# Two-block transformer step: the opening by feature quarters, with the modulation weights stationary and both token blocks fetched first

## Chip, cores and metric

One core of a Trainium2 chip runs the kernel. The metric is the device time of one execution in microseconds.

## What is computed

Two transformer blocks over 256 tokens of 1024 features follow one another. The change touches only the start of the first one. Its layer begins, for the tokens `x` and for the context `ctx` (256 tokens each), with

```
mod_lat = jnp.split(jax.nn.silu(c) @ w_ada[l] + b_ada[l], 6, axis=-1)
mod_ctx = jnp.split(jax.nn.silu(c_ctx)[None, :] @ w_ada[l] + b_ada[l], 6, axis=-1)
sh1, sc1, gt1, sh2, sc2, gt2 = mod_lat
sh1c, sc1c, gt1c, sh2c, sc2c, gt2c = mod_ctx
pl = project(modulate(rmsnorm(x, g_mix[l]), sh1, sc1), w_in[l], w_dec_up[l], b_dec[l])
pc = project(modulate(rmsnorm(ctx, g_mix[l]), sh1c, sc1c), w_in[l], w_dec_up[l], b_dec[l])
```

where `modulate(h, shift, scale)` is `h * (1 + scale) + shift` by feature, and `project` multiplies by `w_in` (queries, keys, values, gates, a convolution's inputs, and 32 columns `dd` that `w_dec_up` expands into decays). A gated linear attention in both directions over chunks of 64 tokens, a convolution branch and a SwiGLU follow; then the second block with two attentions and two SwiGLUs. All is float32.

## The kernel before

**Products.** A float32 product with weights of `w_in` is made of three: weights and activations are each split into a high part (rounded by ScalarE, `whi`, `A_hi`, `B_hi`) and a remainder (a subtraction on VectorE, `wlo`, `A_lo`, `B_lo`), and high x high, high x low and low x high are summed in PSUM (`three`, L1274). A is the tokens' side, B the context's. A "unit" is 256 columns of a weight matrix, 1 MiB; unit u lives in slot u % 3 of the rings `raw`, `whi`, `wlo`. SP (the queue that issues most transfers) loads it (`load_unit`), ScalarE and VectorE each `split` it, TensorE multiplies. The order of the units is `P1` (L43): dd is unit 0, k0 and k1 are 1 and 2, v0 to v3 are 3 to 6, q0 and q1 are 7 and 8; dd, k and v run for both sides.

**The opening (L1737 to 1771 on TensorE).** Shift and scale of the first norm are 2048 columns of `w_ada`, fetched as eight blocks of 256 columns (`ada0`, 1 MiB each) at the head of SP's queue, with the small vectors behind the second and `ctx` and `x` behind the fourth. For each block TensorE keeps two columns (silu of `c` and `c_ctx`) stationary and streams the block's 256 columns, eight products deep. That gives rows; ScalarE copies them to `arow`, and 16 small transposes (L1756) make columns of them, one for each feature group of 128. VectorE's `columns` adds the biases and the norm's gain. In between run the norms: squares on ScalarE, the root on GpSimd (`norm`, L695), the scaling on VectorE, transposes on TensorE (L1340). Then come shift and scale (`modulate` on ScalarE for ctx, `affine` on VectorE for x), the split into high and low, the dd unit, and k0, whole unit after whole unit.

**Behind it.** `gla(u, half)` (L1469) puts attention steps between the halves of the units: after the first half of k0 and of k1, `decay_products` (L1371) expand dd into decay arguments. ScalarE and VectorE make decays of them (`gla_front`: absolute value, exponential, logarithm, scans), each in program order with the splits of coming units. After the first half of v2 and of v3 TensorE transposes the decayed keys of the context and of the tokens (`turn_keys`, L1387), which ScalarE copies out (`ctx_key_tokens`, `key_tokens`).

**Later modulation.** The other norms' shift and scale are computed by GpSimd and VectorE (`adapt`) from further blocks of `w_ada`, and are brought into columns by `shift_and_scale` (L1357): 16 products with 128 columns stationary and a single column of ones moving.

```
for x in range(2):
    for k in range(KD):
        c = UC * ada_pos(NORM_UNITS[n][x]) + P * k
        ins = mm(bank[b][:, KD * x + k:KD * x + k + 1], acc[:, c:c + P], one, True, True)
```

GpSimd's program starts with the norms' roots, then sets constants, then waits for `as_mm` (the transposed rows) to load its first `w_ada` block, and for `hlo_done` 16 to compute with it.

## Time and profile before

| | us |
|---|---|
| median of 3 runs | 1217.5 (1215.88 to 1219.05) |
| profiled execution | 1218.4 |
| its span | 1216.6 |
| TensorE busy | 1166.5 (96%) |
| VectorE busy | 853.4 (70%) |
| ScalarE busy | 574.0 (47%) |
| GpSimd busy | 325.1 (27%) |

A row of the trace begins with the start in us and the duration, then engine, source line and operation, what it writes and reads, the shapes, and how many instructions it merges; behind it in brackets stands the idle time before it and what ended it. PE is TensorE's products and PEld its weight loads, which overlap; DVE is VectorE, ACT ScalarE, POOL GpSimd. A float32 product shows as two rows ("passes"), a product of split parts as one, a transpose as one. PEclk is the clock granted to TensorE as a share of 2.4 GHz; 0.50 is 1.2 GHz. A row of windows has the stretch and its length, the busy time (and instructions) of PE, PEld, DVE, ACT and POOL, then PEclk, the share of the DMA engines and GB/s. Lines L1272, L838 and L1819 are helpers that record many operations: go by the tiles.

### The profile page before, as it was taken

How to read it: one execution, taken by the hardware profiler on the slowest of the kernel's cores; microseconds unless marked ns; L12 is line 12 of the kernel's file. 1: busy time of each engine (PE TensorE's matmuls, PEld its weight loads, DVE VectorE, ACT ScalarE, POOL GpSimd, SP SyncE). 2: the span in 40 equal slices, each digit the busy share in tenths (PEclk: the TensorE clock that was granted, in tenths of full speed). 3: DMA queues.
4: the chain of work that ended last, by engine and by line, in shares of the span. 5: the costliest groups of instructions: out<-in, count | busy, mean ns of one | idle time of the engine just before them, and what ended most of it. 6: DMA issues, size and time to landing. Idle time of an engine off the chain costs nothing.

```text
span 1216.6 us, 18692 instructions
## 1 busy us (share of the span) xinstructions
PE 1166.5 (96%) x7600; PEld 1040.7 (86%) x7600; DVE 853.4 (70%) x935; ACT 574.0 (47%) x734; POOL 325.1 (27%) x219
## 2 busy tenths in 40 slices
PE   6899999999999899999989999999999989999996
PEld 2599988999999888888878888889998989888885
DVE  0478474489577778877778877788766587755676
ACT  1566434354443364444555444445654625544452
POOL 1376573066565200000020000011156663000000
PEclk9899999999999899999989999999999989999999
DMA  9643645365866648777747777755954655656670
GB/s 310 218 139 105 208 144 168 105 217 186 273 232 218 203 169 275 242 254 257 267 147 255 254 252 246 261 161 190 298 181 149 201 186 179 204 177 201 213 258 35
DMA packets 192354, 250.59 MB, mean 206 GB/s; under 512 B 4763, under 2 KB 171870, under 8 KB 192158
## 3 DMA queue, kind: packets, MB, share of 16 engines
q1 hardware_dynamic: 183838, 217.44, 54.9%
q0 software_dynamic: 8448, 32.18, 7.7%
q8 instruction: 50, 0.82, 0.3%
q14 instruction: 18, 0.15, 0.0%
HBM read 248.56 MB, written 1.05 MB: 205 GB/s over the span
## 4 chain that ended last, share of the span: by engine, by line
PE 77%; DVE 13%; ACT 4%; issue 3%; SPq 2%; DMA 1%; POOL 0%; POOLq 0%; DVEq 0%; ACTq 0%
PE twin L1272 74%; DVE arena L1819 4%; DVE wlo L1819 3%; ACT arena L838 2%; DVE arena L1827 2%; SPq L564 1%; DMA raw<-in_w_in 1%; ACT whi L838 1%; PE twin L1340 1%; DVE X L1819 1%; DVE A_both L1819 1%; PE twin L1607 0%; DVE B_lo L1819 0%; DVE X L1827 0%; ACT L838 0%
## 5 line engine op out<-in xcount | busy, mean ns | idle before, releaser
L1272 PE MATMUL twin<-A_both,whi 128*128 128x256 f32 (+1 forms) x2224 | 584.7, 340 | 2.5 <-DVE arena L1819 1.1
L1819 DVE TENSOR_TENSOR wlo<-raw,whi 128x2048 fp32r<-128x2048 f32 x170 | 422.0, 2484 | 158.9 <-ACT whi L838 158.8
L1272 PE MATMUL twin<-A_both,wlo 128*128 128x256 f32 x1640 | 440.1, 281 | 0.0
L838 ACT ACTIVATE whi<-raw 128x2048 fp32r<-128x2048 f32 x170 | 325.1, 1912 | 217.9 <-PE twin L1272 212.1
L1272 PEld LDWEIGHTS twin<-A_both,whi 128*128 128x128 f32 x2224 | 375.1, 191 | 45.9 <-issue 6.7
L1272 PEld LDWEIGHTS twin<-A_both,wlo 128*128 128x128 f32 x1640 | 312.3, 190 | 11.3 <-DVE A_both L1819 0.4
L838 ACT ACTIVATE arena<-twin 128x512 f32<-128x512 f32 (+6 forms) x168 | 88.8, 554 | 125.5 <-PE twin L1272 84.8
L838 ACT ACTIVATE arena<-arena 128x512 f32<-128x512 f32 (+7 forms) x132 | 70.0, 559 | 164.3 <-DVE arena L1819 128.6
L756 POOL TENSOR_TENSOR ada_raw<-ada_raw,arena 128x2048 f32<-128x2048 f32 x24 | 104.7, 4361 | 145.9 <-DMA ada_raw<-in_w_ada 135.0
L1272 PE MATMUL twin<-whi,A_both 128*128 128x256 f32 x640 | 123.9, 295 | 15.4 <-DVE A_both L1819 10.3
L1272 PE MATMUL twin<-whi,B_hi 128*128 128x512 f32 (+2 forms) x340 | 126.8, 373 | 0.2 <-DVE B_lo L1819 0.2
L1272 PE MATMUL twin<-arena 128*2 128x256 f32 (+11 forms) x752 | 115.8, 318 | 11.3 <-DMA arena<-in_w_ada 11.1
L1272 PE MATMUL twin<-wlo,B_hi 128*128 128x512 f32 (+2 forms) x340 | 125.2, 368 | 0.0
L1272 PE MATMUL twin<-whi,B_lo 128*128 128x512 f32 (+2 forms) x340 | 125.2, 368 | 0.0
L1272 PEld LDWEIGHTS twin<-whi,A_both 128*128 128x128 f32 x640 | 105.2, 202 | 17.2 <-DVE A_both L1819 10.7
L1272 PEld LDWEIGHTS twin<-arena 128*128 128x128 f32 (+6 forms) x752 | 79.6, 155 | 39.4 <-issue 15.6
L1819 DVE TENSOR_TENSOR arena<-arena,twin 128x512 f32<-128x512 f32 x92 | 62.3, 684 | 62.4 <-ACT arena L838 49.3
L720 POOL TENSOR_SCALAR arena<-arena 128x1 f32<-128x1 f32 x4 | 1.6, 393 | 375.4 <-ACT arena L838 375.3
L1827 DVE SCALAR_TENSOR_TENSOR arena<-ada_raw,arena 128x256 f32 (+1 forms) x196 | 95.1, 485 | 7.0
L1272 PE MATMUL twin<-wlo,A_both 128*128 128x256 f32 x320 | 93.4, 292 | 0.0
L1272 PEld LDWEIGHTS twin<-whi,B_lo 128*128 128x128 f32 x340 | 64.2, 189 | 11.3 <-issue 0.7
L1272 PEld LDWEIGHTS twin<-wlo,B_hi 128*128 128x128 f32 x340 | 64.2, 189 | 10.7
(128 smaller groups left out, 1203.7 us busy)
## 6 DMA issues: line engine op xcount, KB each, us to landing
raw<-in_w_in SPq DMA_DIRECT2D x49, 1024.0 KB, 5.8
raw<-in_ffn_w_in SPq DMA_DIRECT2D x44, 1024.0 KB, 5.1
ada_raw<-in_w_ada POOLq DMA_DIRECT2D x28, 1024.0 KB, 6.2
ada_raw<-in_w_ada SPq DMA_DIRECT2D x24, 1024.0 KB, 5.4
raw<-in_w_ffn_in SPq DMA_DIRECT2D x22, 1024.0 KB, 5.1
raw<-in_ffn_w_out SPq DMA_DIRECT2D x22, 1024.0 KB, 5.0
raw<-in_w_ffn_out SPq DMA_DIRECT2D x11, 1024.0 KB, 5.1
arena<-in_w_ada SPq DMA_DIRECT2D x8, 1024.0 KB, 11.9
```

Source lines behind the costliest of these rows:

```text
L564: sp.dma_start(ada0[j], a["w_ada"][0].rearrange("(p k) n -> p k n", k=KD)[:, :, UC * j:UC * j + UC])\
L720: link(nc.gpsimd.tensor_scalar(p[0], p[0], EPS, None, ALU.add))
L756: link(nc.gpsimd.tensor_tensor(v[:], v[:], c3[:, :, s:s + 1].to_broadcast([P, KD, UC]), ALU.mult))
L838: return nc.scalar.activation(o, i, f, **kw)
L1272: return nc.tensor.matmul(o, l, r, start=start, stop=stop, **kw)
L1340: ins = nc.tensor.transpose(bank[norm_bank(n, b)][:, c:c + P], src[:, t, P * k:P * k + P], ident)
L1819: return nc.vector.tensor_tensor(o, x, y, op)
L1827: return nc.vector.scalar_tensor_tensor(out=o, in0=x, scalar=sc, in1=y, op0=op0, op1=op1)
```

## The change

- SP's order is `ctx`, the small vectors, `x`, then `w_ada` blocks 0, 4, 1, the dd unit, k0, and blocks 5, 2, 6, 3, 7. The dd unit is fetched 128 columns wide instead of 256, and only its 32 used columns are split.
- The work goes by four quarters of the features (two groups of 128). Block q holds the shift and block q + 4 the scale of quarter q. `start_columns` on TensorE makes columns directly: the block's 128 columns of weights are stationary, and the two columns of `c3` move; 16 products for a block. Rows, `arow` and its transposes are gone.
- For each quarter VectorE makes shift and scale, ScalarE (ctx) and VectorE (x) apply them, and split. TensorE adds that quarter's part of the dd product (`decay_part`, 12 products) and of all of k0 (`key_part`, 24 products).
- ScalarE and VectorE split k1 (`split(2)`) ahead of the fourth quarter.
- `decay_products` for the first two groups come after all of k0 instead of after its first half. The key transposes and their copies come one unit later (context) and half a unit to a unit later (tokens).
- GpSimd sets its constants ahead of the two norms, and its first `w_ada` load waits for the last columns.

```diff
         if n == 0:
-            b = [0, 7] if kind == "dd" else [0]
+            b = [0]
...
+                width = P if kind == "dd" else UC
+                return cview(w, c0 + UC * n, width), KD, width
...
-            for j in range(8):
-                if j == 2:
-
...
+            def load_start(j):
                 sp.dma_start(ada0[j], a["w_ada"][0].rearrange("(p k) n -> p k n", k=KD)[:, :, UC * j:UC * j + UC])\
                     .then_inc(start_ada[j], 16)
-                if j == 3:
-                    sp.dma_start(ctxX, a["ctx"].rearrange(tok, p=P)).then_inc(x_in[0], 16)
-                    sp.dma_start(X[:], a["x"].rearrange(tok, p=P)).then_inc(x_in[1], 16)
+
+            sp.dma_start(ctxX, a["ctx"].rearrange(tok, p=P)).then_inc(x_in[0], 16)
+            for name, r0 in VEC.items():
+                v = a[name]
+                n = math.prod(v.shape) // P
+                src = bass.AP(tensor=v.tensor, offset=0, ap=[[P, n], [1, P]])
+                sp.dma_start(vrows[r0:r0 + n, :], src).then_inc(vec_in, 16)
+            for name, r0, n in (("b_ada", 0, 48), ("b_ada_2", 48, 72)):
+                src = bass.AP(tensor=a[name].tensor, offset=0, ap=[[P, n], [1, P]])
+                sp.dma_start(brows[r0:r0 + n, :], src).then_inc(vec_in, 16)
+            sp.dma_start(X[:], a["x"].rearrange(tok, p=P)).then_inc(x_in[1], 16)
+            load_start(0)
+            load_start(4)
+            load_start(1)
+            load_unit(0, *P1[0])
+            load_unit(1, *P1[1])
+            for j in (5, 2, 6, 3, 7):
+                load_start(j)
 
             for u, (kind, n) in enumerate(P1):
-                load_unit(u, kind, n)
+                if u >= 2:
+                    load_unit(u, kind, n)
...
+        def dd_part(v):
+            return v[:, 0:KD * P].rearrange("p (k w) -> p k w", k=KD)[:, :, 0:2 * RANK]
+
...
+        def start_turned(n, q):
+
+            return 2 * n + q + 1 if q < 2 else 2 * q + n + 1
+
         def norm_bank(n, b):
 
-            return {0: (4, 5, 6, 0), 1: (1, 2, 3, 4), 2: (5, 6, 7, 2), 5: (4, 6, 7, 2)}.get(n, (4, 5, 6, 2))[b]
+            return {0: (1, 2, 1, 2), 1: (4, 7, 4, 7), 2: (5, 6, 7, 2), 5: (4, 6, 7, 2)}.get(n, (4, 5, 6, 2))[b]
 
...
-                    pool.wait_ge(as_mm, 1)
+                    pool.wait_ge(start_cols, 4)
...
+            def start_quarter(q):
+
+                h, ks = start_h[1][q], slice(2 * q, 2 * q + 2)
+                act.wait_ge(start_mod, q + 1)
+                act.wait_ge(tr_done, start_turned(0, q))
+                for m in range(2):
+                    k = 2 * q + m
+                    ins = run(h[:, m, :], bank[norm_bank(0, q)][:, T * m:T * m + T], ACT.Identity,
+                              bias=shift[:, 1, k:k + 1], scale=scale[:, 1, k:k + 1])
+                ins.then_inc(h_done, 1)
+                act.wait_ge(h_done, q + 1)
+                run(B_hi[:, ks, :], h).then_inc(hhi_done, 1)
+                act.wait_ge(h_dve, q + 1)
+                run(A_hi[:, ks, :], start_h[0][q]).then_inc(hhi_done, 1)
+
...
-                if u == U_V + 2:
+                if u == U_V + 3:
                     for g in range(4):
                         ctx_key_tokens(g)
-                if u == U_V + 3:
+                if u == U_Q:
                     for g in range(4):
                         key_tokens(g)
 
...
-            act.wait_ge(ada0_mm, 1)
-            run(arow[:, 0:512], bank[0][0:2, :]).then_inc(ada0_row, 1)
             squares(1)
-            for b in range(1, 4):
-                if b == 3:
-                    split(0)
-                    split(1)
-                act.wait_ge(ada0_mm, b + 1)
-                run(arow[:, 512 * b:512 * b + 512], bank[b][0:2, :]).then_inc(ada0_row, 1)
-            modulate(0)
-            modulate(1)
+            act.wait_ge(landed[0], 16)
+            run(dd_part(whi[0]), dd_part(raw[0])).then_inc(hi_ready, 1)
+            start_quarter(0)
+            split(1)
+            start_quarter(1)
+            start_quarter(2)
+            split(2)
+            start_quarter(3)
 
             for u in range(N1):
                 if u:
                     evac1(u - 1)
-                split(u + 2)
+                    split(u + 2)
...
-                if (u, half) == (U_V + 2, 0):
+                if (u, half) == (U_V + 3, 0):
                     pe.wait_ge(ek_done, 4)
                     for g in range(4):
                         turn_keys(g, Eb[g], ktc_tr)
-                if (u, half) == (U_V + 3, 0):
+                if (u, half) == (U_V + 3, 1):
                     for g in range(4):
                         pe.wait_ge(ktc_sb, g + 1)
                         turn_keys(g, Lb[g], kt_tr)
...
+            def start_columns(j):
+
+                x, q = divmod(j, 4)
+                if q and x == 0:
+                    pe.wait_ge(start_mod, q)
+                pe.wait_ge(start_ada[j], 16)
+                for m in range(2):
+                    c = 2 * (KD * x + 2 * q + m)
+                    for k in range(KD):
+                        ins = mm(bank[3][:, c:c + 2], ada0[j][:, k, P * m:P * m + P], c3[:, k, 0:2],
+                                 k == 0, k == KD - 1)
+                if x:
+                    ins.then_inc(start_cols, 1)
+
+            def start_turn(n, *quarters):
+
+                src = norm_source(n)
+                for t in range(TT):
+                    pe.wait_ge(xn_done, 2 * n + t + 1)
+                    for q in quarters:
+                        if q >= 2:
+                            pe.wait_ge((h_done, h_dve)[n], q - 1)
+                        for m in range(2):
+                            k = 2 * q + m
+                            c = T * m + P * t
+                            ins = nc.tensor.transpose(bank[norm_bank(n, q)][:, c:c + P], src[:, t, P * k:P * k + P],
+                                                      ident)
+                        if t == TT - 1:
+                            ins.then_inc(tr_done, 1)
+
+            def decay_part(q):
+
+                wh, wl = dd_part(whi[0]), dd_part(wlo[0])
+                if q == 0:
+                    pe.wait_ge(lo_ready, 1)
+                    pe.wait_ge(vec_done, 1)
+                for s, x in ((1, B), (0, A)):
+                    pe.wait_ge(hlo_done, 4 * q + (2 if s else 4))
+                    for k in (2 * q, 2 * q + 1):
+                        ins = three(bank[0][0:2 * RANK, T * s:T * s + T], (wh[:, k, :], wl[:, k, :]),
+                                    (x[0][:, k, :], x[1][:, k, :]), True, k == 0 and s == 1, k == KD - 1,
+                                    skip_group_check=True)
+                if q == 3:
+                    ins.then_inc(unit_used, 1)
+
+            def key_part(q):
+
...
+                b = BANKS1[1]
+                for x, o in ((B, bank[b[1]]), (A, bank[b[0]])):
+                    for half in range(2):
+                        for k in (2 * q, 2 * q + 1):
+                            ins = step_product(1, o[:, T * half:T * half + T], x, half, False, k,
+                                               k == 0 and half == 0, None, False)
+                if q == 3:
+                    ins.then_inc(unit_used, 1)
+
             pe.wait_ge(c_silu, 1)
-            for j in range(8):
-                if j == 4:
...
-                if j == 6:
-                    norm(0)
-                pe.wait_ge(start_ada[j], 16)
-                for k in range(KD):
-                    ins = mm(bank[j // 2][0:2, UC * (j % 2):UC * (j % 2) + UC], c3[:, k, 0:2], ada0[j][:, k, :],
-                             k == 0, k == KD - 1)
...
-            norm(1)
+            pe.wait_ge(ident_done, 1)
+            pe.wait_ge(vec_in, 16 * (len(VEC) + 2))
+            nc.tensor.transpose(bank[6][:, 0:NVEC], vrows[0:NVEC, :], ident[0:NVEC, 0:NVEC])
+            nc.tensor.transpose(bank[6][:, P:P + BROWS], brows[0:BROWS, :], ident[0:BROWS, 0:BROWS])\
+                .then_inc(vec_tr, 1)
+            start_turn(0, 0, 1)
+            start_columns(0)
+            start_turn(1, 0, 1)
+            start_columns(4)
+            start_columns(1)
+            decay_part(0)
+            start_columns(5)
+            key_part(0)
+            start_columns(2)
+            start_turn(0, 2)
+            start_turn(1, 2)
+            decay_part(1)
+            start_columns(6)
+            key_part(1)
+            start_columns(3)
+            start_turn(0, 3)
+            start_turn(1, 3)
+            start_columns(7)
+            decay_part(2)
+            key_part(2)
+            decay_part(3)
+            key_part(3)
+            gla(U_K, 0)
 
...
+            def start_columns(q):
+
+                k = slice(2 * q, 2 * q + 2)
+                v = bank[3][:, 0:32].rearrange("p (x k s) -> p x s k", x=2, s=2)
+                both = [P, 2, 2]
+                dve.wait_ge(start_cols, q + 1)
+                if q == 0:
+                    dve.wait_ge(vec_done, 1)
+                tt(shift[:, :, k], v[:, 0, :, k], bcol[:, 2 * q:2 * q + 2].unsqueeze(1).to_broadcast(both), ALU.add)
+                c = KD + 2 * q
+                link(tt(scale[:, :, k], v[:, 1, :, k], bcol[:, c:c + 2].unsqueeze(1).to_broadcast(both), ALU.add))
+                g = VEC["g_mix"] + 2 * q
+                stt(scale[:, :, k], scale[:, :, k], 1.0, vec[:, g:g + 2].unsqueeze(1).to_broadcast(both),
+                    ALU.add, ALU.mult).then_inc(start_mod, 1)
+
+            def start_quarter(q):
+
+                ks = slice(2 * q, 2 * q + 2)
+                start_columns(q)
+                dve.wait_ge(start_mod, q + 1)
+                dve.wait_ge(tr_done, start_turned(1, q))
+                for m in range(2):
+                    k = 2 * q + m
+                    ins = ts(start_h[0][q][:, m, :], bank[norm_bank(1, q)][:, T * m:T * m + T],
+                             scale[:, 0, k:k + 1], shift[:, 0, k:k + 1], ALU.mult, ALU.add)
+                ins.then_inc(h_dve, 1)
+                for s, (hi, lo) in ((1, (B_hi, B_lo)), (0, (A_hi, A_lo))):
+                    dve.wait_ge(hhi_done, 2 * q + (1 if s else 2))
+                    rest(lo[:, ks, :], start_h[s][q], hi[:, ks, :]).then_inc(hlo_done, 2)
+
...
-            split(0)
-            dve.wait_ge(vec_done, 1)
-            columns(0, 7, VEC["g_mix"], 0, (0, 1))
-            for b in range(4):
-                low(0, b)
-                dve.wait_ge(tr_done, 4 + b + 1)
-                for k in (2 * b, 2 * b + 1):
-                    ins = affine(1, k)
-                ins.then_inc(h_dve, 1)
-            for b in range(4):
-                low(1, b)
+            dve.wait_ge(hi_ready, 1)
+            rest(dd_part(wlo[0]), dd_part(raw[0]), dd_part(whi[0])).then_inc(lo_ready, 1)
+            start_quarter(0)
             split(1)
+            start_quarter(1)
+            start_quarter(2)
+            split(2)
+            start_quarter(3)
 
             for u in range(N1):
                 if u:
                     evac1(u - 1)
 
                 gla_step(2 * (u - 1 - U_Q) + 1)
-                split(u + 2)
+                if u:
+                    split(u + 2)
```

## Rows read from the trace of the kernel before

**Rows 1.** The page: span, engines' busy times, TensorE's clock in 40 slices.

```profile
span 1216.6 us, 18692 instructions
...
PE 1166.5 (96%) x7600; PEld 1040.7 (86%) x7600; DVE 853.4 (70%) x935; ACT 574.0 (47%) x734; POOL 325.1 (27%) x219
...
PEclk9899999999999899999989999999999989999999
```

**Rows 2.** Timeline of TensorE in the opening: start us, duration us, instruction, count.

```profile
9.12 16.45 PE L1272 MATMUL twin<-arena 128*2 128x256 f32 x64 [9.12 <-DMA arena<-in_w_ada]
...
14.19 10.88 PEld L1272 LDWEIGHTS twin<-arena 128*2 128x2 f32 x51 [0.29 <-issue]
...
45.40 0.90 PE L1756 MATMUL twin<-arena,ada_raw 2*128 2x2 f32 x12
...
51.68 0.56 PE L1272 MATMUL twin<-B_hi,whi 128*128 128x256 f32 x1
...
67.90 3.72 PE L1272 MATMUL twin<-arena 32*128 32x256 f32 x16
```

**Rows 3.** Timeline of three engines behind the opening, and one row of windows.

```profile
69.07 3.43 ACT L838 ACTIVATE arena<-twin,arena 128x256 f32<-128x256 f32 x8 [5.50 <-PE twin L1272]
...
119.56 2.28 DVE L1819 TENSOR_TENSOR wlo<-raw,whi 128x2048 fp32r<-128x2048 f32 x1
...
122.03 0.47 PE L1272 MATMUL twin<-whi,A_both 128*128 128x256 f32 x2 [3.10 <-ACT arena L838]
...
120.00:125.00 5.00, 2.97 (x19) 3.00 (x20) 5.00 (x5) 5.00 (x8) 4.63 (x3) 0.84 0.35 104
```

**Rows 4.** Timeline of SP, ScalarE and VectorE in the opening.

```profile
3.57 1.15 SPq L560 DMA_DIRECT2D arena<-in_g_mix  x1
...
8.16 1.25 SPq L564 DMA_DIRECT2D arena<-in_w_ada  x2
...
41.40 1.91 ACT L838 ACTIVATE whi<-raw 128x2048 fp32r<-128x2048 f32 x1 [4.20 <-DMA raw<-in_w_in]
...
44.78 1.91 ACT L838 ACTIVATE whi<-raw 128x2048 fp32r<-128x2048 f32 x1 [1.47 <-DMA raw<-in_w_in]
...
47.73 0.24 DVE L1819 TENSOR_TENSOR arena<-twin,arena 128x8 f32<-128x8 f32 x2 [2.10 <-PE twin L1756]
...
50.34 0.69 DVE L1819 TENSOR_TENSOR B_lo<-arena,B_hi 128x512 fp32r<-128x512 f32 x1 [1.82 <-ACT B_hi L838]
...
50.95 0.99 DVE L1824 TENSOR_SCALAR arena<-twin,arena 128x256 f32<-128x256 f32 x2
```

**Rows 5.** Timeline of TensorE: three places with the passes of `shift_and_scale`.

```profile
420.29 3.65 PE L1272 MATMUL twin<-arena 128*128 128x1 f32 x32
...
811.01 3.63 PE L1272 MATMUL twin<-arena 128*128 128x1 f32 x32
...
1014.09 3.63 PE L1272 MATMUL twin<-arena 128*128 128x1 f32 x32
```

**Rows 6.** Windows around these places and in the opening, and transposes behind one.

```profile
55.00:56.00 1.00, 0.99 (x7) 0.79 (x6) 1.00 (x3) 0.75 (x3) 0.00 (x0) 0.94 0.00 0
...
424.00:426.00 2.00, 2.00 (x11) 2.00 (x11) 0.38 (x4) 0.00 (x0) 0.18 (x1) 0.50 1.09 371
...
811.00:813.00 2.00, 2.00 (x20) 1.99 (x18) 1.93 (x4) 1.14 (x4) 0.68 (x2) 1.00 0.90 356
...
1017.60:1019.00 1.40, 1.40 (x9) 1.40 (x9) 1.07 (x4) 0.00 (x0) 0.87 (x1) 0.53 1.00 381
...
423.80 3.58 PE L1340 MATMUL twin<-arena 128*128 128x128 f32 x16
```

**Rows 7.** Timeline of TensorE's weight loads in the opening, two single loads.

```profile
52.05 0.33 PEld L1272 LDWEIGHTS twin<-B_hi,wlo 128*128 128x128 f32 x1
...
55.24 0.19 PEld L1272 LDWEIGHTS twin<-B_hi,wlo 128*128 128x128 f32 x1
```

**Rows 8.** Timeline of GpSimd: the head norm of the attention.

```profile
244.10 0.30 POOL L683 TENSOR_SCALAR arena<-arena 128x4 f32<-128x4 f32 x1 [45.74 <-ACT arena L838]
```

110 lines of the change are left out of this document (23 added, 87 removed).

## Prediction

> **What bounds the kernel now.** Of the page I read first the shares and the slices [rows 1]: TensorE is busy for 96% of 1216.6 us, and only the first two of 40 slices fall short (6 and 8 tenths, clock 9 and 8 tenths). So the rest is TensorE's own time, and an opening that is N us shorter or longer moves everything behind it by N, unless a wait further on takes it up. The timeline of the opening shows what it is made of [rows 2]: TensorE starts at 9.12 when the first block of w_ada lands, and is in w_ada passes, transposes and waits until 51.68, when the decay product starts. At 67.90 come the first `decay_products` (16 passes over 32 rows).
>
> That 67.90 is my **reference point**, because a serial chain starts there: ScalarE's Abs, Exp and Ln from 69.07, VectorE's scans, up to the low half of unit 5's weights at 119.56; TensorE resumes at 122.03 after 3.10 us idle [rows 3]. From 67.90 to 122.03 are 54.1 us, in which TensorE has 51.0 us of work. Before the change the second half of k0 lies in it (48 products, 5.8 us at 0.12, more at the low clock); after it all of k0 lies ahead of the reference point. The chain does not get shorter by that: the idle time at unit 5 grows from 3.1 to some 9 or 10 us, and unit 5 starts 54.1 us behind the reference point in both kernels. Hence: **change of the time = shift of the first `decay_products`**.
>
> **When the weights come.** The first block of w_ada (1 MiB) is used at 9.12; the dd unit, the eleventh MiB, at 41.40, the k0 unit at 44.78, both by a ScalarE that had waited for them [rows 2, 4]. That is (41.40 - 9.12)/10 = 3.23 us for each MiB. The two token blocks now come first, so the first w_ada block lands third: 9.12 + 2 x 3.23 = 15.6. SP issues eleven small transfers between ctx and x, which took 4.6 us of it (3.57 to 8.16) [rows 4]; one MiB covers only 3.2 of these, and I put the first w_ada block at 16.6 (15.6 to 17.6). The last block is at 11.5 MiB: 43.9 to 46. Transfers of MiB 3 to 12 arrive every 3.2 us.
>
> **TensorE's part, step by step.** The eight w_ada blocks cost 128 passes of 0.213 us before (51 in 10.88, at full clock), 27 us [rows 2]. Now each block is 16 products with 128 columns of weights stationary and two columns moving. The nearest row is `shift_and_scale`, the same with one moving column: 16 products stand as 32 passes and take 3.63 to 3.65 us, 0.114 each, at full clock [rows 5]. Eight blocks: 8 x 3.65 = 29.2 us. So at full clock the column products win nothing over the row products, but drop the transposes of `arow` and the last copy between them (45.40 to VectorE's first use at 47.73, 2.3 us) [rows 2, 4].
>
> But the clock does not stay full. Behind the stretches at 420.29 and 1014.09 the granted clock halves: 0.50 in 424 to 426, 0.53 in 1017.6 to 1019 [rows 5, 6]. TensorE was issuing passes without a gap, and it halved all the same. In the opening it also begins at the low level: the first 13 of 64 passes take 16.45 - 10.88 = 5.6 us, 0.43 each, twice the later 0.213 [rows 2]. In the new order there are column stretches from the first block on, with few dense products between them, so I take the opening to be at the low level (1.2 GHz) except behind dense pieces.
>
> What does a column pass cost there? No row shows one. From below it is 0.114 (if the load does not slow down), 3.65 a block; from above double, 7.3. The nearest rows are single loads of 128 columns: 0.33 us at the low level (52.05), 0.19 at the full one (55.24) [rows 7]. The load is longer by 0.14, more than a whole pass of 0.114, so I take it to double. I take 0.216, just under the double: 6.9 a block.
>
> The Trainium skill, page "TensorE: Matmul & The Clock Gate", section "LDWEIGHTS (loading the stationary operand)", states that a load takes its columns over 1.2 GHz, with no mention of the clock level. By that (an estimate) the low level would leave the block at 3.65, and the sum below would give 74 to 77 rather than 91. The load's 0.33 against 0.19 speaks against it [rows 7]. It is the second rival.
>
> The sum at the low level, from 16.6: columns 8 x 6.9 = 55.3; 24 transposes at 0.224 (16 took 3.58) = 5.4 [rows 6]; decay product 4 x 12 and k0 4 x 24, 144 products of 256 columns, which stream for 0.213 as above, with their step 0.215 = 31.0; TensorE waits twice about 0.8 us, once for the first quarter's shift and scale (VectorE's operations from 47.73 on [rows 4]), once for the dd evacuation ahead of `decay_products` = 1.6. End 109.9. The eight transposes of ctx fall into the wait for the first block. At full clock, everything but the columns halved: 16.6 + 29.2 + 24 x 0.112 + 144 x 0.12 + 1.6 = 67.4.
>
> Dense pieces bring the clock back: in the decay product it rose at about 55.1 (0.94 over 55 to 56) [rows 6]. Once full, it stays so through most of a stretch of columns of 3.65 us (420.29 to 423.94) [rows 5], and each us at full clock does the work of two. Four dense pieces lie between the blocks (12 products, 24, 12, 24): I count 3.4 us for each, 13.6. The last piece is 72 products without a block between: 4.5 us at the low level (21 products), then 51 x 0.12 = 6.1 instead of 11.0, 4.9 saved (0.12 is the 0.215 at twice the clock, and a little). 109.9 - 13.6 - 4.9 = **91.4**.
>
> **The other parts.** *VectorE and ScalarE* need, for a quarter, the shift and scale (about 0.6), two affines 0.99, and a hi and two los on 512 columns, 0.7 each: 3.7 us [rows 4], under TensorE's next blocks; only the last one could show, and 36 products (7.7 us) stand before its first use. *ScalarE's `split(2)`* waits ahead of the fourth quarter for the k1 weights, 12.5 MiB, at about 48; TensorE reaches the seventh column block after 75, so nothing waits for that. Without this cover it would cost, see the fifth rival. *The narrower dd unit* saves half a MiB and most of one split (2.3 us VectorE, 1.9 ScalarE): hidden. *GpSimd*: constants ahead of the norms, a few us, in its idle time before the norms. Its first ada load waits for the last columns rather than `as_mm`, so it slides with TensorE by about as much; its slack is 45.7 us idle before the head norm at 244.10 [rows 8]. *The key transposes* go one unit later (32 of them, the same work). The second set is now copied by ScalarE in q0, behind v3's evacuation and one split (1.91 [rows 4]), and its first user comes in q1, 5.8 us of products later. Cost nothing; if that cover were gone, 1 to 2 us. In the idle time at unit 5 the clock falls, but it did so before (0.84 in 120 to 125) [rows 3].
>
> **Result.** Shift 91.4 - 67.9 = +23.5. The profiled execution was 1218.4 with a span of 1216.6, and becomes 1241.9; the median of the runs shown is 0.9 lower: **1241**.
>
> **The rivals.** (1) The forecast: low clock, loads doubled. If two more or two fewer pieces lift the clock, 1234 to 1248; with the start at 15.6 or 17.6, one more either way: 1233 to 1250. Chance 0.57. (2) Low clock, but loads keep their time: a block costs 3.65, the sum at the low level is 16.6 + 29.2 + 5.4 + 31.0 + 1.6 = 84, less four pieces of dense work only (about 1 us each) and 4.9: 74 to 77, +6 to +9, 1223 to 1227. For it: no row shows a column pass at the low level; against: the load's duration. 0.20. (3) The clock stays full, since dense products lie among the columns: dense products end at 811.01, and it stood at 1.00 over 811 to 813, all columns [rows 5, 6]. Reference point 67.4: 1217, no change. Against: the start has no dense work for some 15 us. 0.08. (4) The clock never comes back before the last piece: 109.9 - 4.9 = 105, 1255. 0.06. (5) **Faster**: the transfers, not TensorE, set the end. Last weights at 45 to 48, `split(2)` 1.9 + 2.3 [rows 3, 4], the quarter 3.7, the last 36 products 4.3, the dd evacuation 0.8: 59 to 61, shift -7 at 61, 1210.5. It decides if TensorE's own sum comes to less than 61, that is if a column pass is under 0.09 us and the clock is full; for it, loads that overlap; against, all three rows of 0.114 [rows 5]. 0.09.
>
> **How the numbers follow.** The likeliest is (1), 1241. A range of 1221 to 1251 holds (1) and (2), 0.77, and a little of the cases beside them; I take 1221 to 1252. A measurement of this kernel tells 0.3% (3.7 us) from no change: within it lies (3) and an edge of (2), 0.10; faster is (5), 0.09; slower is the rest, 0.81.
>
> **What the profile after would show.** Column groups (128 x 2 moving) of 32 passes, 6.9 us where the clock reads 0.50, 3.65 where it reads 1.00: this tells (1) from (2). TensorE hardly idle between 17 and 90. First 32-row passes at 91, unit 5's start 54 behind them, with near 10 us idle. The last w_ada block landed 30 us before its use. The prediction is wrong if the clock reads 1.00 over 25 to 70, or if TensorE there waits for w_ada.

## The result and the profile after

The change makes the kernel slower: median 1243.85 us (4 runs, 1241.95 to 1247.81) against 1218.28 (4 runs, 1215.88 to 1220.97) beside it on the same chip, a ratio of 1.0197 (95% interval 1.0164 to 1.0230). The forecast was 1241 in a range of 1221 to 1252. The profiled execution took 1244.9 with a span of 1243.2, 26.6 us above [rows 1].

Lines of the page after (shares, tenths of TensorE's busy time and of its clock in 40 slices):

```profile
PE 1184.7 (95%) x7712; PEld 1078.4 (87%) x7712; DVE 854.8 (69%) x941; ACT 570.8 (46%) x729; POOL 319.9 (26%) x219
...
PE   5998799999999799999989999999999989999997
...
PEclk9979899999999899999989999998999989999999
```

TensorE is again busy 95% of the time; of the 26.6 us, 18.2 are more busy time of its own (1184.7 against 1166.5), although the number of passes is nearly the same. The timeline of TensorE in the opening tells why; its columns are those of [rows 2]:

```profile
15.02 1.11 PE L1754 MATMUL twin<-arena 128*128 128x128 f32 x4 [0.36 <-DVE arena L1877]
15.93 6.82 PE L1272 MATMUL twin<-arena 128*128 128x2 f32 x32
22.61 1.95 PE L1754 MATMUL twin<-arena,X 128*128 128x128 f32 x8
24.35 6.83 PE L1272 MATMUL twin<-arena 128*128 128x2 f32 x32
31.70 6.98 PE L1272 MATMUL twin<-arena 128*128 128x2 f32 x32 [0.52 <-DVE arena L1881]
...
41.09 6.82 PE L1272 MATMUL twin<-arena 128*128 128x2 f32 x32
...
53.03 3.97 PE L1272 MATMUL twin<-arena 128*128 128x2 f32 x32
...
60.77 3.91 PE L1272 MATMUL twin<-arena 128*128 128x2 f32 x32
68.75 3.63 PE L1272 MATMUL twin<-arena 128*128 128x2 f32 x32
...
73.15 5.86 PE L1272 MATMUL twin<-arena 128*128 128x2 f32 x32
...
90.00 3.72 PE L1272 MATMUL twin<-arena 32*128 32x256 f32 x16
```

These are the last transposes of ctx, the eight column blocks with the transposes of x behind the first, and, last, the first `decay_products`. The first four blocks take 6.8 to 7.0 us each, the next three 3.6 to 4.0, the last 5.9: 44.8 us together. The same 32 passes take 0.213 us each in one group and 0.114 in another. Two rows of windows (stretch, busy of PE, PEld, DVE, ACT, POOL, then PEclk, DMA share, GB/s) show the two levels of the granted clock, one between two of the faster blocks, one inside the second of them:

```profile
58.00:60.00 2.00, 2.00 (x11) 1.67 (x10) 0.00 (x0) 0.00 (x0) 0.00 (x0) 0.50 0.00 0
...
62.00:64.00 2.00, 2.00 (x20) 2.00 (x19) 0.00 (x0) 0.00 (x0) 0.00 (x0) 0.99 0.00 0
```

The reference point has moved from 67.90 to 90.00, by 22.1 us, and nothing behind it takes that up. Unit 4 and unit 5 start like this, against the one wait of 3.10 in [rows 3]:

```profile
127.66 0.77 PE L1272 MATMUL twin<-whi,A_both 128*128 128x256 f32 x2 [6.89 <-ACT arena L849]
...
144.80 0.48 PE L1272 MATMUL twin<-whi,A_both 128*128 128x256 f32 x2 [3.38 <-ACT arena L849]
```

Unit 5 is 22.8 us later than before (122.03). From there to 868.12 (845.55 before) the distance stays between 22.5 and 22.8. The other 4 us of the 26.6 arise in the second block's attention and the stage behind it, where the change touches nothing; the experiments come to them.

### The profile page after: what moved, and what is told of

Its sections match the earlier page's. It is cut to its first block, busy times and chain, and to the rows that moved or that the text cites. A ratio compares the mean times of both kernels' runs of the same rounds, so it can differ in the third digit from the quotient of the medians.

```text
span 1243.2 us, 18933 instructions
## 1 busy us (share of the span) xinstructions
PE 1184.7 (95%) x7712; PEld 1078.4 (87%) x7712; DVE 854.8 (69%) x941; ACT 570.8 (46%) x729; POOL 319.9 (26%) x219
## 4 chain that ended last, share of the span: by engine, by line
PE 80%; DVE 13%; ACT 4%; issue 3%; SPq 0%; POOL 0%; DMA 0%; POOLq 0%; DVEq 0%; ACTq 0%
PE twin L1272 77%; DVE arena L1873 4%; DVE wlo L1873 4%; ACT arena L849 2%; DVE arena L1881 2%; ACT whi L849 1%; PE twin L1333 1%; DVE X L1873 1%; DVE arena L2129 0%; DVE arena L2131 0%; PE twin L1754 0%; PE twin L1599 0%; DVE X L1881 0%; DVE A_both L1873 0%; ACT L849 0%
## 5 line engine op out<-in xcount | busy, mean ns | idle before, releaser
L1272 PE MATMUL twin<-A_both,whi 128*128 128x256 f32 (+2 forms) x2224 | 584.5, 340 | 1.2 <-DVE arena L1873 1.1
L1873 DVE TENSOR_TENSOR wlo<-raw,whi 128x2048 fp32r<-128x2048 f32 (+1 forms) x170 | 424.5, 2498 | 165.7 <-ACT whi L849 165.6
L1272 PE MATMUL twin<-A_both,wlo 128*128 128x256 f32 (+1 forms) x1640 | 440.0, 281 | 0.0
L849 ACT ACTIVATE whi<-raw 128x2048 fp32r<-128x2048 f32 (+1 forms) x170 | 323.6, 1904 | 221.5 <-PE twin L1272 212.8
L1272 PEld LDWEIGHTS twin<-A_both,whi 128*128 128x128 f32 (+1 forms) x2224 | 374.0, 190 | 44.8 <-issue 6.8
L1272 PEld LDWEIGHTS twin<-A_both,wlo 128*128 128x128 f32 (+1 forms) x1640 | 311.1, 190 | 11.7 <-DVE A_both L1873 0.6
L1272 PE MATMUL twin<-whi,A_both 128*128 128x256 f32 x640 | 125.6, 298 | 23.2 <-DVE A_both L1873 10.7
L849 ACT ACTIVATE arena<-twin 128x512 f32<-128x512 f32 (+5 forms) x167 | 88.8, 557 | 113.7 <-PE twin L1272 92.2
L1272 PE MATMUL twin<-arena 128*128 128x2 f32 (+9 forms) x880 | 128.6, 302 | 0.5 <-DVE arena L1881 0.5
L1272 PEld LDWEIGHTS twin<-arena 128*128 128x128 f32 (+5 forms) x880 | 113.7, 200 | 9.0 <-DVE arena L1881 0.6
L768 POOL TENSOR_TENSOR ada_raw<-ada_raw 128x1024 f32<-128x1024 f32 x24 | 79.4, 3306 | 1.9
```

The lines of the kernel that those rows point to most:

```text
L768: link(nc.gpsimd.tensor_tensor(v[:, 0:4, :], v[:, 0:4, :], v[:, 4:8, :], ALU.add))
L849: return nc.scalar.activation(o, i, f, **kw)
L1272: return nc.tensor.matmul(o, l, r, start=start, stop=stop, **kw)
L1873: return nc.vector.tensor_tensor(o, x, y, op)
```

## The experiments

My theory: the opening is TensorE's own time, and what makes it long is the low clock, which doubles a column pass (I take its length to be that of its weight load). Rivals: the transfers' new order, the cutting into quarters with its waits, or the chain behind the opening. "Before" beside the runs was 1219.4, 1225.3, 1218.5 and 1223.8 us (medians of 13 runs in each of four sets); single executions of it lie between 1215.7 and 1227.6, and the shortest has a mean granted clock of 0.980, the longest of 0.974. Where only a single time is given, I go by landmarks of the trace rather than by the time.

**Half of the column work.** Each column product is summed over four of its eight feature groups only, so the modulation is left half computed.

```
-                    for k in range(KD):
+                    for k in range(KD // 2):
```

> The changed kernel with the second half of each column product left out (features 4 to 7 of each partition's eight are not summed into shift and scale). Theory (TensorE sets the opening's end, and a column pass costs its weight load): the eight blocks took 44.8 us in the changed kernel, so the first decay_products moves from 90.0 to 65 to 69, and the time falls by 21 to 25 us, to about 1220. Rival (the opening is set by the chain of quarters, or by transfers and the split of k1 ahead of the fourth quarter, not by the columns): the first decay_products stays at 88 to 90, time within 2 us of the changed kernel.

Measured 1212.99 us (about 1220 expected), first decay products at 63.14, 2 us earlier than the theory's range. The blocks, now of 16 passes, on TensorE's timeline:

```profile
15.93 3.41 PE L1272 MATMUL twin<-arena 128*128 128x2 f32 x16
...
38.39 1.84 PE L1272 MATMUL twin<-arena 128*128 128x2 f32 x16
42.41 1.84 PE L1272 MATMUL twin<-arena 128*128 128x2 f32 x16
47.07 1.84 PE L1272 MATMUL twin<-arena 128*128 128x2 f32 x16
49.69 2.46 PE L1272 MATMUL twin<-arena 128*128 128x2 f32 x16
```

Half of the passes is 22.4 us of 44.8, yet the reference point came 26.9 us earlier than in the changed kernel (90.00). The remaining 4.5 us I put down to the clock: from the block at 38.39 on, the third quarter's, it falls back once (the last block takes 2.46 instead of 1.84), where the changed kernel fell back three times (0.50 over 57.2 to 60.5, 64.1 to 67.3 and 74.3 to 84.3 us). The column work carries the loss; with transfers, quarters and waits unchanged, those rivals fall as the main cause.

**Key products behind the decays.** `key_part(0)` to `key_part(3)` leave the quarters and follow in one piece after the first `decay_products`.

```
-            key_part(0)
...
-            key_part(3)
             gla(U_K, 0)
+            for q in range(4):
+                key_part(q)
```

> The changed kernel with all four parts of k0 behind the first decay_products. Theory: 17.5 us of dense products leave the path ahead of the first decay_products, but the clock now has only the short decay parts to come back by, so columns that took 3.6 to 4.0 us take near 6.8 again and give back some 9 us: first decay_products at 80 to 86, time 1232 to 1238. Rival (clock and dense pieces have nothing to do with each other, columns keep their times of 3.6 to 4.0 from the fifth block on): first decay_products at 72 to 74, time about 1224.

Measured 1236.75. TensorE has 96 products less ahead of the reference point, 11.5 us at full clock, and gains 2.4: it comes at 87.55, a little later than the 80 to 86 that I had written, but far from the rival's 72 to 74. The sixth, seventh and eighth block now read

```profile
59.40 6.82 PE L1272 MATMUL twin<-arena 128*128 128x2 f32 x32
66.74 6.99 PE L1272 MATMUL twin<-arena 128*128 128x2 f32 x32 [0.52 <-DVE arena L1879]
...
75.32 6.83 PE L1272 MATMUL twin<-arena 128*128 128x2 f32 x32
```

All eight are at the low level. So it is the pieces of 24 key products that bring the clock back in the changed kernel; the pieces of 12 decay products alone don't here. Dense work among the columns has a price below its own length.

**Rows instead of columns, all else as in the change.** The same quarters, transfers and order; each block is again two silu columns stationary and 256 columns of weights moving, with a copy and four small transposes for each quarter.

```
-                        ins = mm(bank[3][:, c:c + 2], ada0[j][:, k, P * m:P * m + P], c3[:, k, 0:2], ...
+                    ins = mm(bank[0][2 * RANK:2 * RANK + 2, UC * x:UC * x + UC], c3[:, k, 0:2],
+                             ada0[j][:, k, :], k == 0, k == KD - 1, skip_group_check=True)
```

> The changed kernel with the same order of transfers, quarters and units, but each w_ada block again multiplied as rows (two columns stationary, 256 moving), copied by ScalarE for each quarter and turned by four small transposes. Theory (the stationary weights are what costs, since their passes do not hold the clock and are paced by loads): row passes stream and bring the full clock, 3.4 us a block; first decay_products at 69 to 73, time 1219 to 1223. Rival (the tokens ahead of w_ada and the work by quarters cost the 22 us): first decay_products at 85 to 90, time 1238 to 1243.

Measured 1221.86 (1218.44 to 1222.79), ratio 1.0007 (0.9987 to 1.0027): no change against the kernel before. First decay products at 68.39.

```profile
15.94 4.44 PE L1284 MATMUL twin<-arena 128*2 128x256 f32 x16
20.31 1.09 PE L1778 MATMUL twin<-arena,X 128*128 128x128 f32 x8
21.33 3.62 PE L1284 MATMUL twin<-arena 128*2 128x256 f32 x16
...
126.33 0.77 PE L1284 MATMUL twin<-whi,A_both 128*128 128x256 f32 x2 [7.13 <-ACT arena L852]
```

A block is 16 passes here and takes 3.62, and the clock is up within the first (4.44). This is the cleanest split of the change at the reference point: quarters, tokens first and the key products ahead cost 0.5 us; swapping the operands costs the other 21.6. At full clock both forms take the same 3.6 us. What differs is the clock they run at. Further on the split shifts: unit 5 starts at 126.33 behind a wait of 7.13 for ScalarE, 4.3 us later than in the kernel before and 18.5 earlier than in the changed one, so in these three executions some 4 us belong to the new order and the quarters from there on. The spans (1220.6 against 1216.6 and 1243.2) say the same; over all runs the interval leaves room for 3 us at most.

**Filler.** Behind each half block, four products of a matrix of ones with 256 columns of w_ada, into an unused part of the bank (and one wait for the ones at the start).

```
+                    for _ in range(4):
+                        ins = mm(bank[3][:, 128:384], ones[:], ada0[j][:, 0, :], True, True)
```

> The changed kernel with four products of 256 moving columns added behind each of the 16 half blocks of columns: only work added (27 us at the full clock), whose results nobody reads. Theory (the clock falls because column passes stream next to nothing): with streaming among them the clock comes up with the first blocks, every column half block takes 1.8 us (3.6 for a block), and the added work is nearly paid by it: first decay_products at 93 to 99, time 1246 to 1252. Rival (the column passes are slow for another reason than the clock): they stay at 3.4 us a half block wherever they were, first decay_products at 115 or later, time above 1265.

Measured 1250.66, first decay products at 97.92: as expected.

```profile
15.91 3.41 PE L1272 MATMUL twin<-arena 128*128 128x2 f32 x16
19.18 3.76 PE L1272 MATMUL twin<-arena,ones 128*128 128x256 f32 x8
22.74 1.97 PE L1272 MATMUL twin<-arena 128*128 128x2 f32 x16
24.57 1.97 PE L1272 MATMUL twin<-arena,ones 128*128 128x256 f32 x8
```

After the first filler every column pass of the opening is at 0.115 to 0.13: the 16 half blocks take 31.4 us instead of 44.8 (3.41 + 1.97 + 2.08 + 13 x 1.84). The clock fell back once (0.50 over 36.7 to 40), and there it met a filler. The fillers themselves are 35 us, so the exchange doesn't pay, but it turns the clock with the column products, their loads and the transfers unchanged: the low level is the cause of the doubled pass.

**The kernel before with tokens first.** `ctx` and `x` go ahead of the eight w_ada blocks.

```
+            sp.dma_start(ctxX, a["ctx"].rearrange(tok, p=P)).then_inc(x_in[0], 16)
+            sp.dma_start(X[:], a["x"].rearrange(tok, p=P)).then_inc(x_in[1], 16)
             for j in range(8):
```

> The kernel before with only the order of transfers changed: both token blocks ahead of all w_ada blocks. Theory (the order costs by itself only the later start of the row passes, and part of that falls into waits that TensorE had anyway): TensorE's first row pass at 15 to 17 instead of 9.1, first decay_products at 70 to 73 instead of 67.9, time 1221 to 1225. Rival (the order costs the whole 6.5 us, as no wait takes it up): 74.4, time 1226. Second rival (hidden): 68, time as before.

Measured 1223.84 (single). First decay products at 66.48, 1.4 us earlier than before, not 2 to 5 later: TensorE starts at 12.94 instead of 9.12, but from there on waits for no block. The order of the transfers costs nothing in the opening. The span of this execution (1222.0) is 5.4 us longer all the same, though well within what single executions of the kernel before take. About half of it arises at a wait further on (2.80 at 173.19, for two VectorE operations that took 6.88 beside a GpSimd multiplication of 4.66), and the other 3 us right behind that wait, where the granted clock is 0.50 over 174 to 180 against 1.00 at the same work before. The wait belongs to the theory on GpSimd below.

**Columns with w_ada first.** Blocks 0 and 4 are fetched and multiplied ahead of the tokens and the small transposes.

```
+            load_start(0)
+            load_start(4)
             for name, r0 in VEC.items():
...
             pe.wait_ge(c_silu, 1)
+            start_columns(0)
+            start_columns(4)
```

> The changed kernel with w_ada blocks 0 and 4 ahead of the token blocks in SP's queue and on TensorE; all else as changed. Theory: TensorE starts its columns at 9 instead of 15.9 and works without a wait from there, so the first decay_products moves from 90.0 to 83 to 85, time 1236 to 1240. Rival (a later wait, for the small vectors, the tokens' norms or the fifth transfer, takes the gain): 88 to 90, time as changed.

Measured 1238.81; first decay products at 92.71, 8 us later than my theory and 2.7 later than in the changed kernel.

```profile
8.94 13.78 PE L1272 MATMUL twin<-arena 128*128 128x2 f32 x64 [8.94 <-DMA arena<-in_w_ada]
22.58 0.37 PE L1793 MATMUL twin<-arena 75*128 75x75 f32 x1
...
26.40 1.12 PE L1754 MATMUL twin<-arena 128*128 128x128 f32 x4 [3.25 <-DVE arena L1877]
...
31.73 6.83 PE L1272 MATMUL twin<-arena 128*128 128x2 f32 x32
```

TensorE begins 7 us sooner, but the norms need the transposed vectors of 22.58, which now stand behind 13.8 us of columns. TensorE waits for what follows from them (3.25 us ahead of the transposes of ctx, here and in the changed kernel), and the third block starts at 31.73, against 31.70 in the changed kernel. The rival (a later wait takes the gain) was right; the 2.7 us more come behind 31.73 from the same work, at a lower clock (the last block takes 6.82 instead of 5.86).

**Rows, w_ada first, keys last.** Row products, feature quarters, keys behind the decays, and the splits of units 1 and 2 behind the quarters. Against the row variant above:

```
             pe.wait_ge(c_silu, 1)
+            start_rows(0)
+            start_rows(4)
             pe.wait_ge(ident_done, 1)
...
             gla(U_K, 0)
+            for q in range(4):
+                key_part(q)
```

> A version built on what was found: row passes (as before), w_ada blocks 0 and 4 first, work by quarters (as changed), all of k0 behind the first decay_products, splits of k0 and k1 behind the last quarter, k0's weights last among these transfers, split of v0 behind the logarithms. Theory (the chain from the first decay_products sets unit 5's start, so everything not needed for it leaves its path): first decay_products at 50 to 54, unit 5 at 104 to 111 (54 to 57 later; TensorE has as much work in between), time 1202 to 1210. Rival (moving k0 behind it only makes TensorE the bound of that stretch, and the gain is given back): first decay_products at 50 to 54 but unit 5 at 116 or later, time 1212 or more.

Measured 1217.53 (1214.73 to 1221.59), ratio 0.9950 (0.9925 to 0.9975). First decay products at 65.38 instead of the 50 to 54 that I wrote. The cause is that of the run before: rows 0 and 4 end at 18.3, then the norms are waited for, and the third block starts at 28.49. The time is the rival's (1212 or more): at the `shift_and_scale` passes of 420.29 in the kernel before, this one stands at 422.57.

**Rows, tokens first, keys last.** The same in the change's order of transfers and work.

```
             start_turn(0, 0, 1)
+            start_rows(0)
             start_turn(1, 0, 1)
+            start_rows(4)
...
+            for q in range(4):
+                key_part(q)
```

> Row products, feature quarters, transfers and order of work as in the changed kernel (tokens first), all key products behind the first decay products, the splits of units 1 and 2 behind the quarters. My theory, that TensorE's own work sets the first decay products: 68.39 of the row variant with keys between, less 96 key products at 0.12, 11.5, so 56 to 60; then the chain behind it of 54 to 58 us gives a shift of -8 to -11 and 1208 to 1213. The rival, that something else is then last (the chain of ScalarE and VectorE with its splits, as where the row variant had its chain at 57.9 instead of 54.1): first decay products at 56 to 60 as well, but the time at 1214 to 1219.

Measured 1217.00 (1213.65 to 1219.81), ratio 0.9974 (0.9950 to 0.9997). First decay products at 62.80, not 56 to 60, behind two waits for the last quarter:

```profile
50.43 3.62 PE L1287 MATMUL twin<-arena 128*2 128x256 f32 x16
...
58.91 0.30 PE L1287 MATMUL twin<-B_hi,whi 128*32 128x256 f32 x1 [3.03 <-DVE B_lo L1902]
...
62.80 7.16 PE L1287 MATMUL twin<-arena 32*128 32x256 f32 x16 [2.19 <-ACT arena L852]
```

Without the key products, ScalarE's and VectorE's work for the last quarter is uncovered: 5.2 us of waits, and the clock falls in them (the decay products take 7.16 instead of 3.72). In the prediction the last quarter was hidden by 36 products in front of its first use; here that cover is gone, and the price is seen. The time is the rival's.

**The kernel before, opening lengthened.** The last block's row product is made seven times over.

```
+                for _ in range(7 if j == 7 else 1):
                     for k in range(KD):
```

> The kernel before, its last w_ada block's row product made seven times over: 6 x 16 = 96 passes more, 0.213 us each at full clock, 20.4 us, all ahead of the last copy of the rows. My theory, that an opening longer by N makes the whole longer by N and nothing more: first decay products at 88.3, unit 5 at 142.4, time 1238 to 1240 (+20 to +22). The rival, that a late opening costs something further on by itself (the changed kernel's span grew by 26.6 where its opening grew by 22.1): +24 or more, 1242 or above. The other rival, slack behind the opening that takes some of it up: under 1236.

Measured 1239.58 (1234.88 to 1243.43), ratio 1.0161 (1.0104 to 1.0218); the profiled execution 1236.1. First decay products at 85.06, 17.2 us later. That is less than the 20.4 us added, since up to the last pair of blocks this execution was already 2.5 us ahead. All later landmarks:

```profile
138.72 0.47 PE L1272 MATMUL twin<-whi,A_both 128*128 128x256 f32 x2 [2.57 <-ACT arena L838]
...
862.93 0.41 PE L1272 MATMUL twin<-whi,B_hi 128*128 128x384 f32 x1 [0.17 <-DVE B_lo L1820]
...
1008.86 0.79 PE L1272 MATMUL twin<-whi,A_both 128*128 128x256 f32 x2 [4.08 <-DVE A_both L1820]
```

Unit 5 is 16.7 later, 862.93 is 17.4 later, 1008.86 (991.23 before) 17.6, the span 17.5. So in this execution a longer opening passes through one to one, and being late costs nothing by itself. The 4 us more of the changed kernel are something else. The four times fall into two pairs, 1234.9 and 1236.1, 1243.1 and 1243.4; of the upper pair there is no trace. The rival's 1242 or above is what two of the four show, so it is excluded for the traced execution only.

**GpSimd's multiplication in four pieces.** Where they arise, the changed kernel has this on VectorE and GpSimd:

```profile
935.88 5.63 DVE L1873 TENSOR_TENSOR wlo<-raw,whi 128x2048 fp32r<-128x2048 f32 x1
...
935.76 3.61 POOL L767 TENSOR_TENSOR ada_raw<-ada_raw,arena 128x2048 f32<-128x2048 f32 x1 [5.53 <-DMA ada_raw<-in_w_ada]
939.44 4.32 POOL L768 TENSOR_TENSOR ada_raw<-ada_raw 128x1024 f32<-128x1024 f32 x1
...
945.98 0.63 PE L1599 MATMUL twin<-arena 128*128 128x128 f32 x4 [2.14 <-ACT arena L849]
...
989.12 5.68 DVE L1873 TENSOR_TENSOR wlo<-raw,whi 128x2048 fp32r<-128x2048 f32 x1 [0.67 <-ACT whi L849]
...
995.55 0.35 PE L1272 MATMUL twin<-B_hi,whi 128*128 128x256 f32 x1 [1.87 <-DVE B_lo L1873]
```

The split takes 2.28 alone. Begun 0.12 us behind GpSimd's multiplication, it took 5.63: until 939.37, where that ended, and then its own 2.28 (3.49 + 2.28 = 5.77, nearly what was measured). GpSimd's next operation, 2.38 alone, took 4.32 and ended 2.25 behind VectorE's. They don't share a rate; each waits for the other's instruction to end. ScalarE's softmax and TensorE wait behind it. The Trainium skill, page "SBUF — State Buffer", section "Who interferes with whom", states this: an operation of VectorE with two SBUF inputs contends with one of GpSimd that reads SBUF, and the ports that the two engines share are an exclusive lock. The trace agrees (5.63 against 2.28). In the kernel before, the same split came at 913.30, ahead of GpSimd's at 914.83, and took 2.28.

This is not all of the 4 us. The changed kernel is 22.6 us behind at 868.12 and 24.8 at 945.98, of which 0.9 is given back by 967. The same meeting comes again at 989.12 (5.68; the split before took 2.29 at 965.17, begun ahead of GpSimd's), and TensorE's wait at 995.55 is 0.8 longer than its counterpart. Behind this wait the clock falls, and it did not before:

```profile
995.70:999.10 3.40, 3.40 (x18) 3.40 (x19) 3.40 (x4) 0.47 (x1) 3.32 (x2) 0.52 0.90 306
```

The same work in the kernel before, 970.80 to 975.00, has a granted clock of 1.00. That is the last 1.8 us. So about half of the 4 us is the clock; that the longer wait let it fall is likely, but not shown. The edit makes the waits shorter:

```
-                link(nc.gpsimd.tensor_tensor(v[:], v[:], c3[:, :, s:s + 1].to_broadcast([P, KD, UC]), ALU.mult))
+                for k in range(0, KD, 2):
+                    link(nc.gpsimd.tensor_tensor(v[:, k:k + 2, :], v[:, k:k + 2, :], c3[:, k:k + 2, s:s + 1]...
```

> The changed kernel, GpSimd's multiplication of 128x2048 in adapt made in four pieces of 128x512. In the second block's attention VectorE's split of 2.28 us took 5.63 at 935.88, begun 0.12 us behind GpSimd's multiplication of 3.61. Theory, that VectorE waits for the end of a GpSimd instruction that is under way: with pieces of about 1 us no split is above some 4 us, TensorE's wait there of 2.14 us falls to 1.3 or less, and the time to 1240 to 1243. The rival, that the two engines only share a rate over their common time: splits of 5 us and more stay, and the time is 1243 to 1246.

Measured 1240.32 (1239.35 to 1241.37), ratio 1.0163 (1.0118 to 1.0207), 3.5 us below the median of the changed kernel. TensorE's timeline:

```profile
415.14 0.50 PE L1274 MATMUL twin<-whi,A_both 128*128 128x256 f32 x2 [0.57 <-DVE A_both L1875]
...
956.23 0.63 PE L1601 MATMUL twin<-arena 128*128 128x128 f32 x4 [0.86 <-ACT arena L851]
...
1030.83 6.99 PE L1274 MATMUL twin<-arena 128*128 128x1 f32 x32 [9.02 <-POOL arena L772]
```

The wait in the attention is 0.86 instead of 2.14, no split there is above 3.1 us, and at 415.14 a wait of 6.31 (at 422.77 in the changed kernel) has shrunk to 0.57. The kernel gains 8 to 9 us on the changed one up to 844 us, and in the second block's attention and the stage behind it, where the changed kernel lost its 4, it gains on: at 1003.77 it is 18.2 ahead. Then it loses most of this: at 1030.83 TensorE waits 9.02 us for GpSimd's last block, and the passes behind that wait run at the low level (6.99 instead of 3.6). Four pieces take GpSimd 4.4 us where nothing meets them and mostly 6.3, at most 8.8, where VectorE works beside it, instead of 3.6 for the one. The span is 5.6 us shorter than the changed kernel's (1237.6). This opening, the same instructions as the change, also ended 3.0 us later (93.00): its last column block stayed at 6.83 us where the other had 5.86. So much can the clock differ for the same code in the opening.

**Pieces in the first transformer block only**, on the kernel before and on the rows with tokens first.

```
+                w = 2 if n < NADA1 else KD
+                for k in range(0, KD, w):
```

> The kernel before, GpSimd's multiplication of 128x2048 in four pieces of 128x512 for the 16 blocks of w_ada of the first transformer block only. In the changed kernel with pieces everywhere the last product stage of the first block began at 415.14 instead of 422.77, 7.6 us earlier (TensorE's wait for VectorE's A_both 0.57 instead of 6.9), and lost it again at 1030.83, where GpSimd was 9 us late. Theory, that VectorE's waits behind long GpSimd instructions cost TensorE that time in any version: start of the same stage at 393 to 395 instead of 400.06, time 1209 to 1213. The rival, that the gain was a matter of how the engines happened to stand to each other in that one kernel: less than 3 us, 1215.5 or above.

(The 6.9 in that text is 6.31, as above.) Measured 1215.70 (1213.63 to 1218.73), ratio 0.9949 (0.9926 to 0.9972). The stage begins at 397.93, not at 393 to 395. The wait there is 1.54 instead of 6.18, but a new one of 4.65 for VectorE came at 131.73. 2.1 us of the 7.6 are left at that stage: closer to the rival. Behind the shorter wait the clock stays up (1.00 over 397 to 403 us, 0.50 in the kernel before), so that the next `shift_and_scale` passes come 3.6 us earlier (416.74 against 420.29).

> The row variant with tokens first and the key products behind the decays (1217.0, its stage at 398.39), with the same four pieces in the first block. Theory: the two gains add up, 1.5 us from the opening and 5 to 8 from the pieces, the stage at 391 to 393, time 1208 to 1212. The rival, that the pieces' gain depends on how the engines happen to stand: 1215 or above.

Measured 1208.73 (1207.60 to 1214.95), ratio 0.9897 (0.9845 to 0.9949): faster than both kernels, the whole interval below 1. The stage begins at 389.34 after 0.44 us of waiting, 10.7 us earlier than in the kernel before. Against the same kernel without pieces that is 9.1 us (398.39), where the pieces gave the kernel before 2.1. What they bring depends on how the two engines stand to each other; that they bring something held in all three kernels, though by 0.3 to 0.8%, with the runs in part taken in different sets.

## Why the prediction was right, point by point

- **Start of the columns.** 16.6 forecast, 15.93 measured, but not by the way of the forecast, the landing of the first w_ada block. TensorE goes from the transposes of ctx at 15.02, which had waited for VectorE (0.36), into the columns without a wait. So the agreement says little about the sum of the transfers. TensorE waits nowhere for w_ada, and the last block stands ready well before 73.15, since the DMA share is down to 0.03 over 50 to 52 us. As expected; the fifth rival (faster, transfers set the end) would have needed the columns in 0.09 us a pass.
- **A column pass at the low level.** The step between two rows, load kept or doubled: 6.9 a block taken, 6.82 measured, 0.213 a pass against 0.114. The load of [rows 7], longer by 0.14 at the low level, was the right row to go by, and the second rival falls. That the pass is as long as its load is argued, not shown: one and two moving columns take the same 0.114. The rule of the Trainium skill, page "TensorE: Matmul & The Clock Gate", section "LDWEIGHTS (loading the stationary operand)", names columns over 1.2 GHz for a load and no clock level; for a pass that doubles with the level the trace doesn't agree, and the measurement decides. The filler run shows it with nothing else changed: 3.41 for 16 passes at the low level, 1.84 to 1.97 at the full one.
- **How often the clock comes back.** Four pieces at 3.4 us, 13.6 off 55.3, were forecast, so 41.7 for the eight blocks; measured 44.8. The sum is near, the count was not: the first piece (12 products) brought nothing, the three blocks behind the second to fourth piece gained 2.9 to 3.3 each, and the last gained 1.0. In the keys-last run the first two pieces of 12 lifted nothing; here the third piece, also 12, did, begun 1 us behind a stretch at the full level. I had counted all four alike.
- **Last piece.** 72 products in 10.6 and a wait of 0.8 forecast; from 79.01 to 90.00 are 11.0. The step of a product of split parts at the low level is 0.213, near the 0.215 taken; the row pass that the prediction likened it to has that length at the full level.
- **Reference point.** 91.4 forecast, 90.00 measured: +23.5 against +22.1. That it is so near is in part luck: the column blocks took 3 us more than forecast, while start, waits, transposes and products together took 4.5 less.
- **The chain behind it.** 54.1 us forecast to unit 5, measured 54.8; idle time 9 to 10 forecast at unit 5, measured 10.3, but 6.9 of it at unit 4, which waits for ScalarE's copy of k1. The chain was right, its place in part: the row variant had 57.9 there, so 54 is not a constant of the chain.
- **Costed at nothing.** Key transposes, GpSimd's later start, the narrower dd, `split(2)`: between unit 5 and 845.55 the shift stays within 0.3 us, so they cost nothing that shows. But the row variant is 4.3 us behind the kernel before at unit 5 and waits there for ScalarE; the order of ScalarE's work is not free once the opening is short.
- **What was missed.** The sum ends 3.0 us short of the profiled execution (1241.9 against 1244.9), or 2.9 of the median. The opening was 1.4 shorter than forecast, the chain 0.7 longer; the missing term is the 4 us between 868.12 and the end, where VectorE's two-input operations and GpSimd's meet differently and the clock falls once more. "Shift of the time = shift of the first decay products" holds where only the opening is lengthened (17.2 to 17.5). Elsewhere the spans depart from it by up to 7 us: tokens first moved the reference point by -1.4 and the span by +5.4, rows with tokens first and keys last moved them by -5.1 and -0.9.
- **My criterion for being wrong** was badly posed. The page's clock reads 1.00 up to 57 us while the passes are 0.213 until 53; it seems to show 1.00 until its first change. Already [rows 2] had this: passes of 0.43 from 9.12 under a clock of 1.00. In an opening the pass's length tells the level, not the clock row.

That it was the operands' exchange and not the quarters was argued in the prediction only by prices; the row variant shows it (68.39 against 90.00; 126.33 against 144.80 at unit 5). Open is what exactly lifts the clock (12 products did once and once not), and whether the last 4 us are in every execution of the changed kernel: its four times spread over 5.9 us, and one was traced.

## What to carry to other kernels

Before making a small product "cheap" by turning it into weight loads with one or two moving columns, ask what clock it will run at: here such passes didn't hold the clock and cost double at the low level, while the same product with the large operand moving cost the same at full clock and kept it. Cut out or repeat the suspected work and follow one landmark through the whole trace; a difference that arises where nothing was changed came here from how VectorE and GpSimd meet, and from the clock behind the wait that this makes. Where GpSimd works on large tiles beside a VectorE on the critical path, shorter GpSimd instructions are worth a try, in the stages where GpSimd has time to lose.

## What the runs showed of the hardware

- TensorE without a gap can still sit at the low clock: from 15.93 to 53 us column passes and short pieces ran at 0.213 us a pass, with 0.5 us of waiting among them. It was up behind each piece of 24 dense products and fell again among the columns and short pieces that followed (0.50 from 57.2 and from 74.3 us); with four products of 256 columns behind each half block it came up at 23 us and fell only once up to 98 us.
- Row passes lifted it at once: after 4.44 us for the first block every further one takes 3.62.
- VectorE and GpSimd exclude each other by instruction (5.63 instead of 2.28 us; 4.32 instead of 2.38), not by sharing a rate. Pieces on GpSimd cost GpSimd itself: 4.4 for four, mostly 6.3 beside VectorE and up to 8.8, against 3.61 for one alone.
- The same opening in two kernels differed by 3.0 us at the reference point through the clock alone, and the position of GpSimd's operations, with the clock behind it, moved the end by about 4 us: such amounts can hardly be forecast from the trace of one execution.
